# Moving the operands of the full-rate matmuls to other addresses modulo 512 bytes

## The reference

```python
def first_block(x, ...):
    for l in range(2):
        h = rms_norm(x, g_mix[l])
        proj = h @ w_in[l]                       # 1024 x 10052, the widest product
        ...                                      # sparse attention, a 31-tap convolution with a
        ...                                      # layer norm, a 3-tap one, stick-breaking attention
        merged = gates[0]*y_a + gates[1]*y_b + gates[2]*y_c + gates[3]*y_d
        x = x + merged @ w_merge[l]
        h2 = rms_norm(x, g_ffn[l])
        gt = causal_dwconv(h2 @ w_ffn_gate[l], ffn_conv_w[l])
        x = x + (silu(gt) * (h2 @ w_ffn_up[l])) @ w_ffn_down[l]     # 2816 wide
    return x

def second_block(x, ...):
    for l in range(2):
        proj = rmsnorm(x, norm_w[l]) @ w_in[l]   # then latent attention, a gated delta rule in
        ...                                      # chunks of 64, block attention with a bias
        x = x + y @ w_out[l]
    return rmsnorm(x, final_norm_w)
```

## Time and profile before

| | |
|---|---|
| median of 3 runs | 1415.04 us (1412.85 to 1418.36) |
| profiled execution | 1406.11 us, span 1404.3 us |
| PE busy | 1361.8 us (97% of the span), 10226 matmuls |
| PEld busy | 1283.6 us (91%) |
| DVE busy | 1054.0 us (75%) |
| ACT busy | 760.8 us (54%) |
| mean granted TensorE clock | 0.993 |
| DMA | 223.90 MB, mean 159 GB/s |

### The profile page before, as it was taken

The page is one execution under the profiler, slowest core; times in us unless marked ns, Lnnn a source line. Parts: engine busy times, 40 slices in busy tenths (PEclk is TensorE's granted clock), DMA queues, the critical chain, the costliest instruction groups (busy, mean ns, idle before and its releaser), DMA issues.

```text
span 1404.3 us, 25372 instructions
## 1 busy us (share of the span) xinstructions
PE 1361.8 (97%) x10226; PEld 1283.6 (91%) x10226; DVE 1054.0 (75%) x1800; ACT 760.8 (54%) x1173; POOL 73.0 (5%) x62
## 2 busy tenths in 40 slices
PE   6999999999999999999999999999999999989998
PEld 6899999998999989999999989999888999889996
DVE  6899898677766676998986777766678756677555
ACT  6454656555544464545556555444585536675353
POOL 0000000000000000000000000000002210003300
PEclk9999999999999999999999999999999999999999
DMA  7565445465556456555355546564544123442122
GB/s 273 180 210 163 138 151 170 161 210 180 181 188 205 150 189 208 180 191 169 99 183 170 205 133 217 195 198 147 196 153 143 52 70 130 149 149 63 61 91 75
DMA packets 108846, 223.90 MB, mean 159 GB/s; under 512 B 6037, under 2 KB 17557, under 8 KB 108601
## 3 DMA queue, kind: packets, MB, share of 16 engines
q1 hardware_dynamic: 106352, 218.93, 47.0%
q10 hardware_dynamic: 2376, 3.35, 0.7%
HBM read 221.21 MB, written 1.06 MB: 158 GB/s over the span
## 4 chain that ended last, share of the span: by engine, by line
PE 42%; DVE 4%; ACT 2%; issue 1%; DMA 1%; ACTq 0%; POOL 0%; DVEq 0%; POOLq 0%
PE bank L481 14%; PE bank L456 8%; PE bank L490 7%; PE bank L503 6%; PE bank L511 3%; PE bank L461 2%; DVE wlo L1719 1%; PE bank L526 1%; DVE w L2242 1%; PE bank L1108 1%; PE bank L1111 1%; ACT whi L1140 1%; ACT hhi L1175 0%; PE bank L533 0%; DMA ring<-in_w_in 0%
## 5 line engine op out<-in xcount | busy, mean ns | idle before, releaser
L1719 DVE TENSOR_TENSOR wlo<-ring,whi 128x1024 fp32r<-128x1024 f32 (+3 forms) x430 | 499.7, 1182 | 195.8 <-ACT whi L1140 174.6
L1140 ACT ACTIVATE whi<-ring 128x1024 fp32r<-128x1024 f32 (+3 forms) x430 | 434.1, 1026 | 374.5 <-PE bank L481 225.2
L481 PE MATMUL bank<-hhi,whi 128*128 128x256 f32 x2016 | 282.0, 282 | 6.8 <-ACT sgb L1398 4.8
L490 PE MATMUL bank<-hhi,wlo 128*128 128x256 f32 x2016 | 278.1, 279 | 0.0
L481 PE MATMUL bank<-hlo,whi 128*128 128x256 f32 x2016 | 276.2, 279 | 0.0
L481 PEld LDWEIGHTS bank<-hhi,whi 128*128 128x128 f32 x2016 | 254.8, 190 | 11.8 <-ACT sgb L1398 5.4
L481 PEld LDWEIGHTS bank<-hlo,whi 128*128 128x128 f32 x2016 | 252.8, 190 | 0.0
L490 PEld LDWEIGHTS bank<-hhi,wlo 128*128 128x128 f32 x2016 | 251.1, 188 | 1.2 <-issue 0.7
L456 PE MATMUL bank<-w 128*128 128x128 f32 (+5 forms) x928 | 131.7, 295 | 2.7 <-ACT w L1532 2.5
L456 PEld LDWEIGHTS bank<-w 128*128 128x128 f32 (+2 forms) x928 | 115.4, 191 | 10.4 <-ACT w L1532 2.9
L2554 POOL TENSOR_TENSOR st<-st,mhalf 128x1 f32<-128x1 f32 (+2 forms) x34 | 35.4, 1042 | 1237.8 <-DVE st L1740 565.3
(11 more groups left out here) (300 smaller groups left out, 1559.1 us busy)
## 6 DMA issues: line engine op xcount, KB each, us to landing
ring<-in_w_in SPq DMA_DIRECT2D x100, 1024.0 KB, 5.1
ring<-in_w_ffn_down SPq DMA_DIRECT2D x22, 1024.0 KB, 5.0
ring<-in_w_ffn_gate SPq DMA_DIRECT2D x20, 1024.0 KB, 5.1
ring<-in_w_ffn_up SPq DMA_DIRECT2D x20, 1024.0 KB, 5.1
ring<-in_w_merge SPq DMA_DIRECT2D x8, 1024.0 KB, 5.0
ring<-in_w_out SPq DMA_DIRECT2D x8, 1024.0 KB, 5.0
ring<-in_w_oc SPq DMA_DIRECT2D x4, 1024.0 KB, 5.0
ring<-in_w_od SPq DMA_DIRECT2D x4, 1024.0 KB, 5.0
```

The lines of the kernel that those rows point to most:

```text
L481: done = e.matmul(o, wh[:, k, cols(u)], s_[:, k0 + k, :], stop=False, skip_group_check=True, start=opens and k == 0 and s_ is sh and u % 2 ...
L490: done = e.matmul(o, wl[:, k, cols(u)], sh[:, k0 + k, :], start=False, stop=closes, skip_group_check=True)
L1140: e.activation(part_of(whi, j), part_raw(j), ACT.Copy).then_inc(*up("hi.a"))
L1719: e.tensor_tensor(part_of(wlo, j), part_raw(j), part_of(whi, j), ALU.subtract).then_inc(*up("lo.v"))
```

## The change

Gaps are allocated in front of five tensors and `cs`, `hhi` and `hlo` change places in the order of allocation. No instruction, wait, transfer or size changes; the sequence on every engine is the same, with other addresses.

```diff
         ring = sb("ring", [P, NSLOT, SLOT])
         whi = sb("whi", [P, NPART, PART], F32R)
+        sb("gap_wlo", [P, 16])
         wlo = sb("wlo", [P, NPART, PART], F32R)
+        sb("gap_hhi", [P, 48])
+        hhi = sb("hhi", [P, 8, S], F32R)
         cs = sb("cs", [P, 2, 48])
+        hlo = sb("hlo", [P, 8, S], F32R)
         posi = sb("posi", [P, 2], I32)
         posf = sb("posf", [P, 2])
-        hhi = sb("hhi", [P, 8, S], F32R)
-        hlo = sb("hlo", [P, 8, S], F32R)
+        sb("gap_cst", [P, 64])
         cst = sb("cst", [P, NCN])
...
         first = ExitStack()
+        first.enter_context(nc.sbuf_tensor("gap_fhi", [P, 112], F32))
         fhi = first.enter_context(nc.sbuf_tensor("fhi", [P, 2, 4, S], F32R))
+        first.enter_context(nc.sbuf_tensor("gap_flo", [P, 24], F32))
         flo = first.enter_context(nc.sbuf_tensor("flo", [P, 2, 4, S], F32R))
         w1 = first.enter_context(nc.sbuf_tensor("w1", [P, 18568], F32))
```

## The result

The change made the kernel slower: 1432.93 us (median of 4 runs, 1431.03 to 1434.47) against 1416.53 us (4 runs), a difference of the medians of 16.4 us; the ratio on record is 1.0137 with a 95% interval of 1.0104 to 1.0169. Forecast was 1397 us, faster, with a range of 1374 to 1430; what happened is rival C's sign with another mechanism.

The account below looks back on a forecast made before the run. TensorE's back-to-back matmul pace was taken to bound the kernel. Between 38 us faster and 25 us slower, half the possible gain, 18 us, came off the 1415 us median: 1397 us, range 1374 to 1430.

Parts of the forecast that it names:

- rival C: In `chans`, all three products: new distances collide and slow the steps; 1440 us, about 1455 with hhi by wlo; chance 0.24.
- What bounds the kernel: TensorE, busy 97% of the span: the time is its back-to-back matmul pace, with two paces, 113.1 and 117.7 ns.
- the choice between the ends: Full-rate matmuls: between 38 us faster and 25 us slower, half of the possible gain was taken, 18 to 19 us.
- the load's floor: Weight load on TensorE, read from one-column matmuls: 112 ns a step, the lower bound for 256-column matmuls.
- The bound on the bad side: Full-rate matmuls without a new conflict: 256-column steps all at 117.8 ns, 21 us more; 512-column at 232, 4 us more.
- Step 3: 416-column parts: distance 192 can cost 5 to 25 ns a step; hhi by wlo priced at 22 us if all paid.
- Rival B: TensorE's streams: starting phase, not operand place, picks the lock, so nothing happens; 1415 us, plus or minus 5; chance 0.27.
- Its sign: Sign of no change: in the profile after, 113.3 and 117.8 ns come back in the same shares.
- Steps 4 and 5: VectorE and ScalarE, `wlo` subtraction at another place: 0; plain float32 matmuls with `w1` at 96: 0, or 4 us either way.

Follow-up runs that it names:

- The sweep: Bare-burst kernel computing nothing of the reference, operand distance 0 to 480 bytes in steps of 32: 113.3 or 117.8 ns a 256-column step at 192 and 448.
- the finer sweep: The same bare bursts with distances 0 to 248 in steps of 8 bytes: no 256-column step below 113.3 ns; 112 has one lock.
- experiment 3: Against the kernel before, only hhi (to 384) and hlo (to 256) moved: ratio 1.018, 1437.99 us.

## Why the prediction was wrong

**What bounds the kernel:** right. TensorE's pace is the time, and the two locks at one clock were a conflict between its own two streams, as read from the earlier trace rows.

**The step that failed** is the choice between the ends: "I take half of the possible gain", on the ground that the present distances "have room to leave that relation". It took two locks as a sign of a poor distance. The sweep shows the contrary: of the places on the 32-byte grid 192 (448) is the one where most bursts take the fast lock (in the finer sweep a single burst at 64 did too), and the others have means of 116.7 to 119.9 ns. So instead of the 18 us taken off, the steps added 25 us. A trace in which every pair stands at one distance cannot say whether that distance is good. Its one honest reading was the excess over the load's floor: 1.3 ns in the fast lock left little to gain for 69% of the steps and much to lose.

**The bound on the bad side**, "all steps at 117.8, 21 us more" and 4 us for 512 columns, missed that other distances have paces of their own, up to 120 ns on the 32-byte grid and 123 off it. That the sum, 25 us, is what the profiled span grew by is luck.

**Step 3** misread: the 210 ns were laid to distance 192, which the sweep shows as the best for 256 columns; hhi by wlo, the very product that I priced at 22 us for standing at 192, was the one that lost nothing (278.1 us before and after). In those parts the activation stays at one place, so own and next distance are the same and only alternate between 64 and 192 with the row of weights. The trace of before has eight such groups of eight: in four of them the last row's two steps take 210 and 197 or 198 ns, in the other four 193 or 194 and 187 or 188, at the same distance of 192. So the distance does not make the 210; what does is not explained.

**Rival C** had the sign and a time near the measured one (1440 against 1433 us), but its geometry was wrong: it put 192 among the bad places, and knew nothing of a period of 256 or of places that are lost four bytes away. **Rival B** failed: the lock is chosen by the starting phase, as it said, but only where the distance has two. Its sign, shares of 69 and 31% that stay, came back in the kernel with all h distances moved by 256 bytes (2085 slow steps against 2103), not in the changed one.

**Steps 4 and 5** were right: line 1719's mean stayed at 1223 ns, and plain float32 matmuls kept one pace at the four distances tried.

The Trainium skill's page SBUF — State Buffer, section "Who interferes with whom", has TensorE's two read ports independent. These runs differ: with no other engine at work the step of a full-rate stream went from 113.3 to 123 ns by the distance of its two operands alone, though what in the memory or the array makes it so is not shown; for plain float32, 215.85 ns at the four distances tried, the rule held. The page TensorE: Matmul & The Clock Gate, section "Wait — 56ns, not 53.3ns?", gives N / 2.4 + 2.5 ns. No full-rate stream here came to the 109.2 and 215.8 ns estimated from that page; the best were 113.3 and 226.7.

## What to carry to other kernels

Where full-rate float32 matmuls run back to back with a weight load each, the allocation order is a tuning knob: between the kernel before and the one with all pairs at 0, TensorE's step of 256 columns goes from 114.7 to 119.9 ns (4.5%) and the whole kernel's time by 1.6%. Check the distance modulo 256 of moving to stationary operand, own and next. Here 192 was the best for 256 columns and 64 within 2 ns of the best for 512; they are one layout, as the operands change roles. 112 looks as good in a bare burst and is worth a try where 256 columns rule. A small tensor inserted between such buffers can cost a per cent without a changed instruction: the 320 and 384 bytes of experiment 3 cost 1.8%. Before forecasting a gain from leaving a state, sweep the alternatives in a bare burst; a single profile of one state says nothing of the others.

## What the runs showed of the hardware

The pace of such a stream locks into repeating patterns: 113.3 ns (113, 113, 114 in turn), or 117.8 ns, or 226, 229 and 232 ns for 512 columns in turn. At distance 192 two locks exist, chosen by the starting phase and kept over a hundred steps (380 and 238 in a row in the profile of before); at 112 all bursts came to the fast one within ten steps. The dependence has a period of 256 bytes, the two best places lie on multiples of 16 bytes and are gone 4 bytes away, and moving both operands together leaves the paces as they are, though not always which lock is taken. The locks nearly repeat between executions (2103 and 2099 slow steps; 94% of the steps to 2 ns), while the clock does not (0.993 and 0.987).
